# Spreading a step's softmax weights over the features: a full-precision product of 2 rows becomes a single-pass product of 34 rows

## The chip, the cores and the metric

The kernel runs on one core of a Trainium2 chip. The metric is the device time of one execution, in microseconds. The core's engines each run their own instruction stream and meet through semaphores: PE (TensorE) multiplies matrices, ACT (ScalarE) and DVE (VectorE) do elementwise work, POOL (GpSimd) builds constants and biases, SP starts transfers.

## The reference, cut to what matters

The program is a chain of transformer layers (two in the first block, two in the second) over 512 tokens of width 1024. The change touches one mixer only, the sparse attention of the first block's second layer. Each of its 16 heads attends in three ways, and a gate for each token and head weighs the three results:

```python
    o_c = jnp.einsum('ghqn,ngd->qghd', p_c, vc)      # 31 compressed keys
    ...
    o_s = jnp.einsum('ghqk,gqkd->qghd', p_s, v_sel)  # selected blocks
    ...
    o_w = jnp.einsum('ghqk,kgd->qghd', p_w, vw)      # window
    g = g_blk.astype(jnp.float32)
    o = g[..., 0:1] * o_c + g[..., 1:2] * o_s + g[..., 2:3] * o_w
```

Here every `p` is a softmax: exponentials divided by their sum. With 512 tokens there are only 8 blocks of 64, so all of them are selected, and both `o_s` and `o_w` are causal attention over all earlier keys.

## The kernel before, in words

All of x stays on chip, transposed (features on the partitions, 512 tokens along the row). Weights arrive in pieces of 128x2048; ACT rounds each to the single-pass format fp32r (L294) and DVE takes the rest (L300), so that a product of nearly full precision is three single-pass products (L304 to L306). Most of the program is such products.

The sparse attention works in 16 steps (`STEPS`), two for each pair of heads: an even step `n` for the selected branch, an odd one for the window. The loop in `pe_nsa`, `act_nsa` and `dve_nsa` runs over `n` and four query tiles `i`, and is pipelined by hand: in round `n` the scores of step `n` are made while the probabilities of step `n-1` are turned and multiplied by the values, and the end of step `n-2` is combined.

- PE: `scores` (L1281) writes a bank, DVE adds the bias and takes the maximum (`masked`, L1510), ACT takes the exponential with its sum (`exps`, L1423). PE turns the probabilities (L1309), ACT and DVE copy them back (L1432, L1559), PE multiplies by the values (`values`, L1325).
- The probabilities aren't normalized. `weigh` (DVE, L1546 to L1550) turns the sums into reciprocals times the gate, two columns of `mt` for the pair's two heads. `turn_small` (PE, L1334) transposes `mt` into bank 7, `take_small` (ACT, L1441) copies it into `ms`, `spread` (PE, L1339) multiplies by the 0/1 matrix `pick`, which repeats each head's row over its 64 features, and `take_spread` (ACT, L1449) copies the result into `oadd`. `combine` (DVE, L1564 to L1571) multiplies the values' product by it and adds.
- For an even step `mt` also holds the compressed branch's 64 columns (`weigh_cmp`, L1533 to L1541, fed by ACT's L1458), so that `take_small` copies 66 rows there and 2 rows for an odd step. PE then multiplies the compressed values with them (`values_cmp`, L1344).

The order on each engine is the order of the code. Two kinds of round alternate. In a round with odd `n`, `spread` serves an odd step (2 rows copied) and DVE also does the compressed branch's weights. In a round with even `n`, `spread` serves an even step (66 rows copied). The output projection (`out_part`, L304 to L306) is woven into the last two rounds.

Of the kernel before, what the change touches and what calls it, by code (L numbers as in the profile page):

```python
# [15 lines left out]
F32R = mybir.dt.float32r  # L16
ACT = mybir.ActivationFunctionType
ALU = mybir.AluOpType
AX = mybir.AxisListType

P = 128
# [3 lines left out]
QT = S // P  # L25
# [5 lines left out]
HEADS, HD, GROUPS = 16, 64, 4  # L31
CMP_LEN, CMP_STRIDE = 32, 16
NC = S // CMP_STRIDE - 1
# [8 lines left out]
def build(nc, a, out):  # L42
    ctx = ExitStack()
    with ctx:
        def sb(name, shape, dt=F32):
            return ctx.enter_context(nc.sbuf_tensor(name, shape, dt))

        def sem(name):
            return ctx.enter_context(nc.semaphore(name))
# [10 lines left out]
        u_hi = nc.alloc_sbuf_tensor_at("u_hi", [P, 4, S], F32R, offset=zone + 16 * S * 4)  # L60
        u_lo = nc.alloc_sbuf_tensor_at("u_lo", [P, 4, S], F32R, offset=zone + 20 * S * 4)
        fsum = sb("fsum", [P, KT, S])
        tmp = sb("tmp", [P, 8, S])
        ident = sb("ident", [P, P])
# [6 lines left out]
        arena = sb("arena", [P, AR])  # L71
        pbank = [ctx.enter_context(nc.psum_tensor(f"bank{i}", [P, S], F32)) for i in range(8)]

        def tiles(at, n, w=S):
            return arena[:, at:at + n * w].rearrange("p (t n) -> p t n", n=w)
# [42 lines left out]
        def chain(ins):  # L118
            act_chain(ins)
# [183 lines left out]
        def three(pe, o, w_hi, w_lo, r_hi, r_lo, first, last):  # L303
            pe.matmul(o, w_hi, r_hi, start=first, stop=False)  # L304
            pe.matmul(o, w_hi, r_lo, start=False, stop=False)  # L305
            return pe.matmul(o, w_lo, r_hi, start=False, stop=last)  # L306
# [788 lines left out]
        mt_dve, mt_pe, ms_act, rr_pe = sem("mt_dve"), sem("mt_pe"), sem("ms_act"), sem("rr_pe")  # L1095
# [3 lines left out]
        o = 0  # L1099
# [18 lines left out]
        rr = arena[:, o:o + 8]; o += 8  # L1118
        bias_h = (tiles(o, 2), tiles(8 * S, 2)); o += 2 * S
        osum, oadd = arena[:, 10 * S:11 * S], arena[:, 11 * S:12 * S]  # L1120
        cs = arena[:, o:o + 8 * (NC + 1)].rearrange("p (h q n) -> p h q n", h=2, q=QT); o += 8 * (NC + 1)
        mt = tiles(o, QT, 2 * (NC + 1) + 2); o += QT * (2 * (NC + 1) + 2)
        pick = arena[2 * (NC + 1):2 * (NC + 1) + 2, o:o + P]; o += P
        csT = arena[:, o:o + S]; o += S
        ms = csT
        cmx = arena[:, o:o + 8]; o += 8
# [13 lines left out]
        VR = 2 * (NC + 1)  # L1140
# [17 lines left out]
        def head_of(n, hd):  # L1158
            return 8 * (n // 2 // 4) + 4 * hd + n // 2 % 4

        def slope_of(h):
            return 2.0 ** (-8.0 * (h + 1) / HEADS)
# [26 lines left out]
        def pool_nsa(e, stage, chain):  # L1189
            e.wait_ge(n_sum, norm_no[stage])  # L1190
            chain(e.memset(tmp[:, :, :], 0.0))
            for h in range(2):
                r = slice(h * HD, h * HD + HD)
                e.dma_start(w1bd[1][r, :, r], NSA_SMALL[1][0][0].rearrange("(l d) e -> d l e", d=HD)).then_inc(small_in, 16)
            e.memset(mt[:, :, :], 0.0)
            chain(e.memset(gz[:, :, NC:NC + 1], 0.0))
            chain(e.memset(pick, 1.0))
            chain(e.affine_select(out=pick, in_=pick, compare_op=ALU.is_ge, fill=0.0, base=0, pattern=[[1, P]],
                                  channel_multiplier=-HD))
            chain(e.affine_select(out=pick, in_=pick, compare_op=ALU.is_ge, fill=0.0, base=HD - 1, pattern=[[-1, P]],  # L1200
                                  channel_multiplier=HD))
            for j in range(PAIRS):
                if j == 1:
                    e.wait_ge(na_dve, 3)
                if j >= 2:
                    e.wait_ge(sc_dve, unit_no[2 * j - 3, 3, 1] + 1)
                for hd in range(2):
                    ins = e.tensor_scalar(bias_h[j % 2][:, hd, :], dist, slope_of(head_of(2 * j, hd)), None, ALU.mult)
                ins.then_inc(bias_pool, 1)
# [3 lines left out]
        def pe_nsa(pe, stage):  # L1213
# [21 lines left out]
            for z in range(2):  # L1235
                ins = pe.transpose(pbank[1][:, z * 32:z * 32 + 32], perow[0:CMP_LEN, z, :], ident[0:32, 0:32])
            ins.then_inc(na_pe, 1)
            pe.wait_ge(na_dve, 1)
            for k in range(KT):
                gk = slice(k * 48, k * 48 + 48)  # L1240
                ins = three(pe, pbank[0][0:48, :], u_hi[:, 0, gk], u_lo[:, 0, gk], h_hi[:, k, :], h_lo[:, k, :], k == 0,
                            k == KT - 1)
            ins.then_inc(na_pe, 1)
            for z in range(2):
                o62 = pbank[2 + z][:, 0:2 * NC].rearrange("p (t n) -> p t n", t=2)
                pe.wait_ge(na_dve, 2 + z)
                for l in range(CMP_LEN):
                    src = (zA, zB)[l // CMP_STRIDE][z]
                    ins = pe.matmul(o62, w1bd[z][:, l, :], src[:, :, l:l + CMP_STRIDE * (NC - 1) + 1:CMP_STRIDE],
                                    start=l == 0, stop=l == CMP_LEN - 1)  # L1250
                ins.then_inc(na_pe, 1)
                if z == 0:
                    pe.wait_ge(na_act, 3)
                    for q in range(QT):
                        ins = pe.transpose(pbank[6][:, q * 48:q * 48 + 48], gT[:, q * P:q * P + P], ident[0:48, 0:48])
# [4 lines left out]
                else:  # L1260
                    pe.wait_ge(na_act, 6)
                    pe.wait_ge(bias_pool, 1)
                    for hd in range(2):
                        r = slice(hd * HD, hd * HD + HD)
                        for t2 in range(2):
                            ins = pe.matmul(pbank[5 + hd][32 * hd:32 * hd + 32, t2 * P:t2 * P + P], gz[r, t2, :], w2bd[r, 1, :],
                                            start=True, stop=True)
# [61 lines left out]
            def turn_small(n):  # L1329
                pe.wait_ge(mt_dve, n + 1)  # L1330
                if n:
                    pe.wait_ge(rs_act, n)
                for q in range(QT):
                    ins = pe.transpose(pbank[7][0:VR + 2, q * P:q * P + P], mt[:, q, :], ident[:, :])  # L1334
                ins.then_inc(mt_pe, 1)

            def spread(n):
                pe.wait_ge(ms_act, n + 1)
                pe.matmul(pbank[7][:, :], pick, ms[VR:VR + 2, :], start=True, stop=True).then_inc(rr_pe, 1)  # L1339

            def values_cmp(n):
                v = unit_no[n, "o"]
# [44 lines left out]
        def act_nsa(e, chain):  # L1387
# [44 lines left out]
                e.activation(probT[hd][:, c:c + nw], pbank[3 + hd][:, 0:nw], ACT.Copy).then_inc(done_, 1)  # L1432

            def take_small(n):
                r = slice(VR * (n % 2), VR + 2)
                e.wait_ge(mt_pe, n + 1)
                if n:
                    e.wait_ge(rr_pe, n)
                if n >= 2 and n % 2 == 0:
                    e.wait_ge(sc_pe, unit_no[n, "o"] + 1)  # L1440
                e.activation(ms[r, :], pbank[7][r, :], ACT.Copy).then_inc(ms_act, 1)  # L1441

            def take_spread(n):
                e.wait_ge(rr_pe, n + 1)
# [26 lines left out]
        def dve_nsa(e, stage, chain):  # L1471
# [17 lines left out]
            for z in range(2):  # L1489
# [3 lines left out]
                for half, dst in ((0, zA[z]), (1, zB[z])):  # L1493
                    for t in range(2):
                        pos = peT[:, z, half * CMP_STRIDE:(half + 1) * CMP_STRIDE].unsqueeze(1)
                        ins = e.tensor_tensor(dst[:, t, :].rearrange("p (n l) -> p n l", l=CMP_STRIDE),
                                              zc[:, 2 * z + t, :].rearrange("p (n l) -> p n l", l=CMP_STRIDE),
                                              pos.broadcast_to([P, S // CMP_STRIDE, CMP_STRIDE]), ALU.add)
# [28 lines left out]
            def gates_of(n, b):  # L1527
                c = 3 * head_of(n, 0) + b
                return gates[:, :, c:c + 13:12]
# [14 lines left out]
            def weigh(n):  # L1544
                e.wait_ge(ex_act, 8 * n + 8)
                chain(e.tensor_scalar(rr, sums[:, n % 2, :], 1e-30, None, ALU.max))  # L1546
                chain(e.reciprocal(rr, rr))
                if n:
                    e.wait_ge(mt_pe, n)
                e.tensor_tensor(mt[:, :, VR:VR + 2], rr.rearrange("p (q h) -> p q h", h=2), gates_of(n, 1 + n % 2),  # L1550
                                ALU.mult).then_inc(mt_dve, 1)

            def take_turned(n, g):
                nw = sum(QT - k for k in GROUPS[g]) * P
# [64 lines left out]
        o = AR - 8 * S - 104  # L1619
# [17 lines left out]
        o = 14 * S  # L1637
# [1133 lines left out]
        def _(pool):  # L2771
            chain = Chain(pool, pool_step)
            for stage, step in enumerate(PLAN):
                enter(pool, stage)
                if step[0] == "setup":
                    pool_setup(pool, chain)
                elif step[0] == "rg":
                    pool_rg(pool)
                elif step[0] == "nsa":
                    pool_nsa(pool, stage, chain)  # L2780
                elif step[0] == "even":
                    pool_even(pool, chain)
                elif step[0] == "odd":
                    pool_odd(pool)
                elif step[0] == "post":
                    pool_owed(pool, stage)
                elif step[0] == "ffn" and FFN[step[1]]["swiglu"]:
                    pool_ffn(pool, step[1])
                elif step[0] == "norm":
                    pool_norm(pool, stage)  # L2790
                    nxt = PLAN[stage + 1]
                    if nxt[0] == "ffn" and FFN[nxt[1]]["swiglu"]:
                        pool.wait_ge(n_add, 7 * norm_no[stage] + 7)
                        pool.memset(fsum[:, :, :], 0.0).then_inc(cleared, 1)
                    if nxt == ("ffn", "f0"):
                        pool_nsa_early(pool, chain)
                    elif nxt == ("ffn", "s00"):
                        pool_even_early(pool, chain)
                    elif nxt == ("ffn", "s10"):
                        pool_odd_early(pool, chain)  # L2800
                leave(pool, "pool")
# [97 lines left out]
```

## Time and profile before

| | us |
|---|---|
| median of 3 runs | 3739.74 |
| lowest and highest | 3736.36 and 3741.02 |
| profiled execution, its time | 3735.31 |
| profiled execution, its span | 3733.6 |
| PE busy | 3529.7 (95%) |
| DVE busy | 1919.1 (51%) |
| ACT busy | 1236.3 (33%) |

The span runs from the first to the last instruction of the trace; the time has a little around it (1.7 us here). A busy share is an average over the whole program; what a change of one stage is worth is read in that stage.

### The profile page before, as it was taken

The page shows a single profiled execution, that of the slowest core. Times are in us where ns is not written, and L with a number is a line of the kernel's source. Part 1 is how long each engine was busy: PE and PEld are TensorE (multiplying, and loading weights), DVE is VectorE, ACT ScalarE, POOL GpSimd, SP SyncE. Part 2 cuts the span into 40 slices and gives each one's busy share as a digit, 9 for nine tenths or more (in the row PEclk, how much of TensorE's full clock was granted, in tenths as well). Part 3 has the DMA queues.
Part 4 walks back from the last instruction along what each step waited for, and adds up shares of the span by engine and source line. Part 5 has one row for each costly group of instructions (what it writes and reads, how often), then busy time and mean ns, then how long its engine had stood idle before and what let it go on. Part 6 is the DMA issues. An engine that isn't in the chain of part 4 may idle for free.

```text
span 3733.6 us, 47718 instructions
## 1 busy us (share of the span) xinstructions
PE 3529.7 (95%) x18695; PEld 2801.1 (75%) x18695; DVE 1919.1 (51%) x2613; ACT 1236.3 (33%) x1717; POOL 512.7 (14%) x400
## 2 busy tenths in 40 slices
PE   6999999899999999999988799999999999989998
PEld 5788888545888878887666678877887777767886
DVE  5655554365555554554566444455445333344455
ACT  3632232365322342223633332233223323232222
POOL 1220002010100041113023021113111100012111
PEclk9999999899999999999999999999999999989999
DMA  3232334100223323232100122232332222212321
GB/s 103 88 107 90 101 98 105 34 1 10 92 90 101 101 81 101 90 101 85 57 25 3 46 79 96 95 101 69 100 101 91 79 79 79 79 57 90 101 90 68
DMA packets 232527, 295.54 MB, mean 79 GB/s; under 512 B 21893, under 2 KB 201464, under 8 KB 232392
## 3 DMA queue, kind: packets, MB, share of 16 engines
q1 hardware_dynamic: 230864, 290.48, 24.2%
q0 software_dynamic: 1152, 3.05, 0.4%
q8 instruction: 96, 1.57, 0.2%
q14 instruction: 39, 0.32, 0.0%
q10 hardware_dynamic: 376, 0.12, 0.0%
HBM read 291.53 MB, written 2.10 MB: 79 GB/s over the span
## 4 chain that ended last, share of the span: by engine, by line
PE 81%; DVE 8%; ACT 5%; issue 3%; POOL 2%; POOLq 0%; DMA 0%; ACTq 0%; DVEq 0%
PE bank L304 23%; PE bank L305 23%; PE bank L306 23%; POOL tmp L636 1%; PE bank L334 1%; PE bank L335 1%; PE bank L333 1%; ACT whi L294 1%; ACT h_hi L550 1%; PE bank L2639 1%; DVE x L681 1%; PE bank L2158 1%; DVE h_lo L665 1%; PE bank L1281 1%; PE bank L1325 1%
## 5 line engine op out<-in xcount | busy, mean ns | idle before, releaser
L304 PE MATMUL bank<-h_hi,whi 128*128 128x512 f32 x2800 | 1118.1, 399 | 53.7 <-DVE h_lo L665 38.2
L305 PE MATMUL bank<-h_lo,whi 128*128 128x512 f32 x2800 | 1101.1, 393 | 0.0
L306 PE MATMUL bank<-h_hi,wlo 128*128 128x512 f32 x2800 | 1100.5, 393 | 0.0
L294 ACT ACTIVATE whi<-raw 128x2048 fp32r<-128x2048 f32 x273 | 521.7, 1911 | 1342.8 <-PE bank L306 1288.3
L300 DVE TENSOR_TENSOR wlo<-raw,whi 128x2048 fp32r<-128x2048 f32 x273 | 632.3, 2316 | 445.6 <-ACT whi L294 445.3
L304 PEld LDWEIGHTS bank<-h_hi,whi 128*128 128x128 f32 x2800 | 533.4, 190 | 186.2 <-issue 71.9
L305 PEld LDWEIGHTS bank<-h_lo,whi 128*128 128x128 f32 x2800 | 533.6, 191 | 114.5 <-issue 5.7
L306 PEld LDWEIGHTS bank<-h_hi,wlo 128*128 128x128 f32 x2800 | 532.4, 190 | 113.2
L304 PE MATMUL bank<-u_hi,whi 128*128 128x512 f32 x1376 | 539.6, 392 | 26.8 <-DVE wlo L300 10.5
L306 PE MATMUL bank<-u_hi,wlo 128*128 128x512 f32 x1376 | 538.6, 391 | 0.0
L305 PE MATMUL bank<-u_lo,whi 128*128 128x512 f32 x1376 | 538.4, 391 | 0.0
L304 PEld LDWEIGHTS bank<-u_hi,whi 128*128 128x128 f32 x1376 | 260.6, 189 | 84.3 <-DVE wlo L300 11.4
L445 POOL TENSOR_TENSOR tmp<-tmp,rstd 128x512 f32<-128x512 f32 x88 | 175.5, 2015 | 1068.1 <-ACT tmp L414 1067.8
L305 PEld LDWEIGHTS bank<-u_lo,whi 128*128 128x128 f32 x1376 | 260.5, 189 | 54.2
L306 PEld LDWEIGHTS bank<-u_hi,wlo 128*128 128x128 f32 x1376 | 260.0, 189 | 54.6
L499 DVE TENSOR_TENSOR fsum<-fsum,bank 128x512 f32<-128x512 f32 x352 | 235.5, 685 | 92.6 <-PE bank L306 92.6
L499 DVE TENSOR_TENSOR x<-x,bank 128x512 f32<-128x512 f32 x256 | 169.6, 684 | 51.0 <-PE bank L306 50.9
L480 DVE TENSOR_TENSOR tmp<-bank,tmp 128x512 f32<-128x512 f32 x88 | 60.9, 692 | 253.1 <-PE bank L306 236.2
L465 DVE TENSOR_TENSOR tmp<-bank,rstd 128x512 f32<-128x512 f32 x88 | 60.1, 691 | 216.3 <-PE bank L306 215.3
L422 ACT ACTIVATE u_hi<-tmp 128x512 fp32r<-128x512 f32 x88 | 55.7, 633 | 336.5 <-DVE tmp L480 336.5
L469 DVE SCALAR_TENSOR_TENSOR tmp<-bank,rstd 128x512 f32<-128x512 f32 x64 | 44.1, 692 | 180.8 <-PE bank L306 180.8
L426 ACT ACTIVATE tmp<-tmp 128x512 f32<-128x512 f32 x64 | 40.5, 632 | 257.2 <-DVE tmp L469 257.2
(398 smaller groups left out, 3048.7 us busy)
## 6 DMA issues: line engine op xcount, KB each, us to landing
raw<-in_ffn_wgu SPq DMA_DIRECT2D x88, 1024.0 KB, 5.0
raw<-in_ffn_wd SPq DMA_DIRECT2D x44, 1024.0 KB, 4.9
raw<-in_mlp_w_up SPq DMA_DIRECT2D x32, 1024.0 KB, 5.3
raw<-in_mlp_w_down SPq DMA_DIRECT2D x32, 1024.0 KB, 5.0
raw<-in_odd_w_in SPq DMA_DIRECT2D x24, 1024.0 KB, 5.1
raw<-in_even_w_in SPq DMA_DIRECT2D x13, 1024.0 KB, 5.3
raw<-in_rg_w_in SPq DMA_DIRECT2D x8, 1024.0 KB, 5.3
raw<-in_odd_w_out SPq DMA_DIRECT2D x8, 1024.0 KB, 5.0
```

Source lines behind the costliest of these rows:

```text
L294: e.activation(whi[:, n % 2, :], raw[:, n % 2, :], ACT.Copy).then_inc(hi_ready, 1)
L300: e.tensor_tensor(wlo[:, n % 2, :], raw[:, n % 2, :], whi[:, n % 2, :].bitcast(F32), ALU.subtract).then_inc(lo_ready, 1)
L304: pe.matmul(o, w_hi, r_hi, start=first, stop=False)
L305: pe.matmul(o, w_hi, r_lo, start=False, stop=False)
L306: return pe.matmul(o, w_lo, r_hi, start=False, stop=last)
L422: e.activation(u_hi[:, u, :], tmp[:, 2 + j, :], ACT.Copy).then_inc(uhi_done, 1)
L426: e.activation(tmp[:, 2 + j, :], tmp[:, j, :], ACT.Square)
L445: e.tensor_tensor(tmp[:, j, :], tmp[:, j, :], rstd[:, :], ALU.mult).then_inc(scaled, 1)
L465: ins = e.tensor_tensor(tmp[:, j, :], pbank[half + j][:, :], rstd[:, :], ALU.mult)
L469: ins = e.scalar_tensor_tensor(tmp[:, j, :], pbank[half + j][:, :], 0.0, rstd[:, :], ALU.max, ALU.mult)
L480: e.tensor_tensor(tmp[:, 2 + j, :], pbank[half + 2 + j][:, :], tmp[:, j, :], ALU.mult)\
L499: e.tensor_tensor(dst[:, m, :], dst[:, m, :], pbank[half + m % 4][:, :], ALU.add)\
```

## The change

The weights are split as the big matrices are: DVE writes the rounded value (fp32r) of each of the two columns into `mt`, and what is left of it into the next column. To have each head's pair of rows beside each other, head 0 has columns `VR` and `VR+1`, head 1 has `VR+32` and `VR+33`; `mt` grows from 66 to 98 columns, and the columns between are zero. `pick` has ones in those four rows and zeros elsewhere, as fp32r, in a free part of `u_lo`. ACT copies 34 rows as fp32r into a free part of `u_hi`, and PE's product takes 34 rows of fp32r operands in one pass. The compressed branch's 64 rows are still copied as full fp32 into `ms`, by an instruction of their own in the even steps.

```diff
--- before.py
+++ after.py
@@ -1119,8 +1119,10 @@
         bias_h = (tiles(o, 2), tiles(8 * S, 2)); o += 2 * S
         osum, oadd = arena[:, 10 * S:11 * S], arena[:, 11 * S:12 * S]
         cs = arena[:, o:o + 8 * (NC + 1)].rearrange("p (h q n) -> p h q n", h=2, q=QT); o += 8 * (NC + 1)
-        mt = tiles(o, QT, 2 * (NC + 1) + 2); o += QT * (2 * (NC + 1) + 2)
-        pick = arena[2 * (NC + 1):2 * (NC + 1) + 2, o:o + P]; o += P
+        mt = tiles(o, QT, 2 * (NC + 1) + 34); o += QT * (2 * (NC + 1) + 34)
+        mt_r = mt.bitcast(F32R)
+        rw = arena[:, o:o + 8]; o += 8
+        pick, msr = u_lo[:, 3, 0:P], u_hi[:, 3, :]
         csT = arena[:, o:o + S]; o += S
         ms = csT
         cmx = arena[:, o:o + 8]; o += 8
@@ -1194,11 +1196,12 @@
                 e.dma_start(w1bd[1][r, :, r], NSA_SMALL[1][0][0].rearrange("(l d) e -> d l e", d=HD)).then_inc(small_in, 16)
             e.memset(mt[:, :, :], 0.0)
             chain(e.memset(gz[:, :, NC:NC + 1], 0.0))
-            chain(e.memset(pick, 1.0))
-            chain(e.affine_select(out=pick, in_=pick, compare_op=ALU.is_ge, fill=0.0, base=0, pattern=[[1, P]],
-                                  channel_multiplier=-HD))
-            chain(e.affine_select(out=pick, in_=pick, compare_op=ALU.is_ge, fill=0.0, base=HD - 1, pattern=[[-1, P]],
-                                  channel_multiplier=HD))
+            pick_f = bias_h[0][:, 0, 0:P]
+            chain(e.memset(pick_f, 0.0))
+            for hd in range(2):
+                ins = e.memset(pick_f[VR + 32 * hd:VR + 32 * hd + 2, hd * HD:hd * HD + HD], 1.0)
+            chain(ins)
+            chain(e.tensor_copy(pick, pick_f))
             for j in range(PAIRS):
                 if j == 1:
                     e.wait_ge(na_dve, 3)
@@ -1331,12 +1334,12 @@
                 if n:
                     pe.wait_ge(rs_act, n)
                 for q in range(QT):
-                    ins = pe.transpose(pbank[7][0:VR + 2, q * P:q * P + P], mt[:, q, :], ident[:, :])
+                    ins = pe.transpose(pbank[7][0:VR + 34, q * P:q * P + P], mt[:, q, :], ident[:, :])
                 ins.then_inc(mt_pe, 1)
 
             def spread(n):
                 pe.wait_ge(ms_act, n + 1)
-                pe.matmul(pbank[7][:, :], pick, ms[VR:VR + 2, :], start=True, stop=True).then_inc(rr_pe, 1)
+                pe.matmul(pbank[7][:, :], pick[VR:VR + 34, :], msr[VR:VR + 34, :], start=True, stop=True).then_inc(rr_pe, 1)
 
             def values_cmp(n):
                 v = unit_no[n, "o"]
@@ -1432,13 +1435,14 @@
                 e.activation(probT[hd][:, c:c + nw], pbank[3 + hd][:, 0:nw], ACT.Copy).then_inc(done_, 1)
 
             def take_small(n):
-                r = slice(VR * (n % 2), VR + 2)
                 e.wait_ge(mt_pe, n + 1)
                 if n:
                     e.wait_ge(rr_pe, n)
                 if n >= 2 and n % 2 == 0:
                     e.wait_ge(sc_pe, unit_no[n, "o"] + 1)
-                e.activation(ms[r, :], pbank[7][r, :], ACT.Copy).then_inc(ms_act, 1)
+                if n % 2 == 0:
+                    e.activation(ms[0:VR, :], pbank[7][0:VR, :], ACT.Copy)
+                e.activation(msr[VR:VR + 34, :], pbank[7][VR:VR + 34, :], ACT.Copy).then_inc(ms_act, 1)
 
             def take_spread(n):
                 e.wait_ge(rr_pe, n + 1)
@@ -1545,10 +1549,12 @@
                 e.wait_ge(ex_act, 8 * n + 8)
                 chain(e.tensor_scalar(rr, sums[:, n % 2, :], 1e-30, None, ALU.max))
                 chain(e.reciprocal(rr, rr))
+                rwq = rw.rearrange("p (q h) -> p q h", h=2)
+                chain(e.tensor_tensor(rwq, rr.rearrange("p (q h) -> p q h", h=2), gates_of(n, 1 + n % 2), ALU.mult))
                 if n:
                     e.wait_ge(mt_pe, n)
-                e.tensor_tensor(mt[:, :, VR:VR + 2], rr.rearrange("p (q h) -> p q h", h=2), gates_of(n, 1 + n % 2),
-                                ALU.mult).then_inc(mt_dve, 1)
+                chain(e.tensor_copy(mt_r[:, :, VR:VR + 33:32], rwq))
+                e.tensor_tensor(mt[:, :, VR + 1:VR + 34:32], rwq, mt[:, :, VR:VR + 33:32], ALU.subtract).then_inc(mt_dve, 1)
 
             def take_turned(n, g):
                 nw = sum(QT - k for k in GROUPS[g]) * P
```

On ACT, at `take_small` of the step with 66 rows in steady state (the round's end, `exps` of query tile 3, then the copies of the turned tiles and the next round's start), there stood before:

```order
L1423 ACTIVATE tmp,arena<-tmp,arena 128x512
L1441 ACTIVATE arena<-bank 66x512
L1432 ACTIVATE tmp<-bank 128x384 x2
L1423 ACTIVATE fsum,arena<-fsum,arena 128x128 x2
L1449 ACTIVATE arena<-bank 128x512
```

and now:

```order
L1426 ACTIVATE tmp,arena<-tmp,arena 128x512
L1444 ACTIVATE arena<-bank 64x512
L1445 ACTIVATE u_hi<-bank 34x512
L1435 ACTIVATE tmp<-bank 128x384 x2
L1426 ACTIVATE fsum,arena<-fsum,arena 128x128 x2
L1453 ACTIVATE arena<-bank 128x512
```

One copy of 66 rows has become two, ahead of the two copies of turned tiles; in the other rounds one copy of 2 rows has become one of 34.

On DVE, at `weigh_cmp` and `weigh` in a round with odd `n` (after `masked` of query tile 1, L1510 before), there stood before:

```order
L1510 ISA arena 128x1
L1533 TENSOR_REDUCE arena<-arena 128x8
L1534 TENSOR_SCALAR arena<-arena 128x8
L1535 RECIPROCAL arena<-arena 128x8
L1537 TENSOR_TENSOR arena<-arena 128x8
L1541 TENSOR_TENSOR arena<-arena 128x4x31 x2
L1546 TENSOR_SCALAR arena<-arena 128x8
L1547 RECIPROCAL arena<-arena 128x8
L1550 TENSOR_TENSOR arena<-arena 128x4x2
L1559 COPY tmp<-bank 128x512
```

and now, from `weigh` on:

```order
L1550 TENSOR_SCALAR arena<-arena 128x8
L1551 RECIPROCAL arena<-arena 128x8
L1553 TENSOR_TENSOR arena<-arena 128x8
L1556 CAST arena<-arena 128x4x2
L1557 TENSOR_TENSOR arena<-arena 128x4x2
L1565 COPY tmp<-bank 128x512
```

Two small instructions are added between the product with the gate and the copy of the turned tile; each of the first four waits for the end of the one before it.

## Rows read from the trace of the kernel before

**Rows 1.** The page: busy time by engine, then the chain's shares by engine.

```profile
PE 3529.7 (95%) x18695; PEld 2801.1 (75%) x18695; DVE 1919.1 (51%) x2613; ACT 1236.3 (33%) x1717; POOL 512.7 (14%) x400
...
PE 81%; DVE 8%; ACT 5%; issue 3%; POOL 2%; POOLq 0%; DMA 0%; ACTq 0%; DVEq 0%
```

**Rows 2.** Busy time by stretch: length, PE busy, granted clock, DMA share, GB/s.

```profile
744.15:768.50 24.35, 22.05 (x137) 1.00 0.00 1
...
792.84:817.42 24.58, 23.34 (x137) 0.93 0.00 1
817.42:842.53 25.11, 23.55 (x136) 0.93 0.00 1
```

**Rows 3.** Groups by form, 703 to 925 us: busy, mean ns, idle before.

```profile
L1339 PE MATMUL bank<-arena 2*128 2x512 f32 x32 | 17.9, 640 | 4.0 <-ACT arena L1441 4.0
...
L1309 PEld LDWEIGHTS bank<-ident,tmp 128*128 128x128 f32 x80 | 9.8, 145 | 0.2 <-DVE tmp L1559 0.2
...
L1334 PEld LDWEIGHTS bank<-ident,arena 128*66 128x66 f32 x64 | 5.8, 112 | 13.0 <-issue 13.0
```

**Rows 4.** Timeline, start of an odd round: start, duration, engine, line.

```profile
743.67 0.87 ACT L1432 ACTIVATE tmp<-bank 128x384 f32<-128x384 f32 x2
...
744.15 1.12 PE L1339 MATMUL bank<-arena 2*128 2x512 f32 x2
...
745.20 0.87 PE L1325 MATMUL bank<-tmp,arena 128*64 128x256 f32 x8
...
746.48 0.39 ACT L1458 ACTIVATE arena<-arena 128x248 f32<-128x248 f32 x1
...
746.74 0.42 DVE L1510 CUSTOM_DVE_ANT_0 fsum<-bank,arena 128x256 f32<-128x256 f32 x1 [1.34 <-PE bank L1281]
...
747.43 0.41 DVE L1533 TENSOR_REDUCE arena<-arena 128x8 f32<-128x248 f32 x1
...
748.31 0.17 DVE L1537 TENSOR_TENSOR arena<-arena 128x8 f32<-128x8 f32 x1
748.52 0.49 DVE L1541 TENSOR_TENSOR arena<-arena 128x124 f32<-128x124 f32 x2
...
749.36 0.17 DVE L1550 TENSOR_TENSOR arena<-arena 128x8 f32<-128x8 f32 x1
749.45 0.69 DVE L1559 COPY tmp<-bank 128x512 f32<-128x512 f32 x1
```

**Rows 5.** Timeline, end of that round and start of the even one.

```profile
755.55 0.58 ACT L1441 ACTIVATE arena<-bank 66x512 f32<-66x512 f32 x1
...
756.03 0.85 ACT L1432 ACTIVATE tmp<-bank 128x384 f32<-128x384 f32 x2
...
756.18 1.12 PE L1339 MATMUL bank<-arena 2*128 2x512 f32 x2 [0.39 <-ACT arena L1441]
...
757.23 0.63 PEld L1325 LDWEIGHTS bank<-tmp,arena 128*64 128x64 f32 x8 [0.76 <-ACT tmp L1432]
...
758.77 0.42 DVE L1510 CUSTOM_DVE_ANT_0 fsum<-bank,arena 128x256 f32<-128x256 f32 x1 [2.29 <-PE bank L1281]
...
760.65 0.69 DVE L1559 COPY tmp<-bank 128x512 f32<-128x512 f32 x1 [0.57 <-PE bank L1309]
```

**Rows 6.** Timeline, the last two rounds, with the output projection.

```profile
915.14 0.40 PE L304 MATMUL bank<-h_hi,whi 128*128 128x512 f32 x1
...
915.37 0.40 PE L305 MATMUL bank<-h_lo,whi 128*128 128x512 f32 x1
...
917.31 0.29 PEld L1339 LDWEIGHTS bank<-arena 2*128 2x128 f32 x2 [0.36 <-issue]
...
918.36 0.87 PE L1325 MATMUL bank<-tmp,arena 128*64 128x256 f32 x8
```

**Rows 7.** Timeline of POOL, the constants and biases before the steps.

```profile
581.76 2.99 POOL L1208 TENSOR_SCALAR arena<-arena 128x512 f32<-128x512 f32 x2
691.68 2.95 POOL L1208 TENSOR_SCALAR arena<-arena 128x512 f32<-128x512 f32 x2 [106.93 <-DVE zadd L1496]
```

## The prediction, made before the result was known

> **What bounds the kernel now.** I read the page first: PE is busy for 95% of the span and holds 81% of the chain that ended last [rows 1]. That speaks for any cut of PE's work. But it is an average, and the change touches only the 220 us of the attention's steps. So I cut these by rounds: two rounds take 24.35 us, in which PE is busy 22.05 us (its modelled ends make that too much) [rows 2]. Then I read the timeline of two rounds for what ends each wait. There PE, ACT and DVE hand the lead to one another: in the middle of an odd round it is DVE's row of small instructions [rows 4], at a round's end it is ACT, for whose copy the product L1339 waits [rows 5], and only in the last two rounds, beside the output projection, does PE have work without a break [rows 6]. So the question is not what PE saves, but what stands in the way of each of the 16 products.
>
> **What PE saves.** The full-precision product is recorded as two instructions, 32 for 16 products, of 640 ns each [rows 3]. From its start to that of the next product it holds PE for 1.05 us (744.15 to 745.20 us) [rows 4]. A single-pass product of 512 columns follows the one before it after 0.23 us and is recorded with 0.40 us [rows 6]. That is the nearest row for the new one; the 34 rows instead of 2 lie on partitions, and the 128-row product has the same length. Two double passes go down to one: 1.05 us is 0.85 us for the columns (four times 0.21) and 0.20 us of handing over, so the new one holds PE for 0.21 + 0.20 = 0.41 us. The saving is 0.64 us, 16 times: 10.2 us at the most, and nothing at the least.
>
> The Trainium skill ("FP8 and Floating Point Precision", the list of FP32 modes) says that true FP32 takes four passes through the array. By it the product is 4 x 0.21 us, which agrees with the 1.05 us once the handing over is taken off.
>
> **What ACT adds.** For an even step one copy becomes two. The copy of 66 rows is recorded with 0.58 us, and the next starts 0.48 us after its start [rows 5]. A copy of 64 or 34 rows has the same columns, so I take 0.48 us for the second; ends: 0.4 us, and 0.58 us if the two don't overlap. For odd steps 2 rows become 34 at the same columns, which I cost at nothing.
>
> **What DVE adds.** `weigh` gets two instructions of 8 elements. The product with the gate, L1550, now has to be waited for; before, the copy of the turned tile started 0.09 us after it (749.36 to 749.45 us). A waited-for one of that size, L1537, lets the next start after 0.21 us (748.31 to 748.52 us) [rows 4]. So the three now take 0.21 + 0.20 + 0.09 = 0.50 us where one took 0.09 us: 0.41 us more in each step. Ends: 0.25 us if the rounded copy is cheap, 0.6 us if writing columns 32 apart or the other format slows them.
>
> By the Trainium skill ("VectorE: DVE Perf Modes", the section on the TRN2 errata) a DVE instruction on SBUF costs 58 cycles plus its elements at 0.96 GHz, 0.07 us for 8 elements, and many small tiles each pay the fixed part. That rule speaks against this change. The trace has 0.17 us for each such instruction, so the rule's figure is too small here and its advice holds more strongly; by its figure the two would add 0.14 us.
>
> **Odd rounds, 7 in steady state [rows 4].** L1339 does not wait for ACT's copy here. At 0.41 us it would end at 744.56 us. L1325 also needs the turned tiles of L1432, which end at 743.67 + 0.87 = 744.54 us, and a semaphore takes 0.05 us (755.55 + 0.58 to 756.18 us [rows 5]): it starts at 744.59 us instead of 745.20 us, 0.61 us early. The scores behind it and DVE's L1510, which waited 1.34 us for them, come as much earlier, at 746.13 us. Then DVE's L1533, 0.69 us behind, would start at 746.82 us; but it needs ACT's L1458, which doesn't wait for PE's product and stays at 746.48 + 0.39 us, plus 0.05: 746.92 us. That is 0.51 us before its 747.43 us. From there on DVE leads without a gap up to L1559, and pays the 0.41 us. Gain: 0.51 - 0.41 = 0.10 us. Queued behind DVE are L1559, `combine` and the next L1510, for which ACT and PE wait, so the rest of the round moves with it.
>
> **Even rounds, 8 [rows 5].** Here L1339 does wait for ACT's copy (0.39 us). Its rows are now the second copy's: it starts 0.48 us later, at 756.66 us, and would let L1325 start at 757.07 us. But behind ACT's copies stand the two copies of turned tiles, L1432: they end 0.48 us later too, at 756.88 + 0.48 = 757.36 us, and L1325 starts at 757.41 us instead of 757.23 us. Loss: 0.18 us. What PE saved is eaten by the extra copy. DVE's 0.41 us lie here in the 0.57 us for which L1559 waits for PE's turned tile, so they cost nothing; with that cover gone they would cost 8 x 0.41 = 3.3 us.
>
> **The last round.** PE's stream is full (0.36 us of issue ahead of L1339, no engine named) and ACT's copy is long done [rows 6]. The projection moves up by the whole 0.64 us.
>
> **The transposes.** `turn_small` loads 98 columns of weights for 66. A load of 66 takes 112 ns, one of 128 takes 145 ns [rows 3], so about 15 ns more, four times a step, hidden in most steps by the bank that PE's scores wait for: 0 to 0.06 us a step, at most 1 us; I take 0.2 us. POOL's constants are made before 582 us, and its next work waits 107 us: nothing [rows 7].
>
> **The sum.** 8 x 0.18 - 7 x 0.10 - 0.64 + 0.2 = +0.3 us. The profiled 3735.31 us become 3735.6 us. That execution lay 4.4 us under the median of 3739.74 us, a tenth of a percent; against the median the forecast is 3740.0 us. No change: less than 0.2% (7.5 us) is about what a measurement of this kernel can't tell from none.
>
> **The rivals.**
>
> *PE's saving comes through everywhere.* If the even rounds' copies were hidden and DVE's two instructions too, all 16 products would give 0.64 us: -10.2 us, 3729.5 us. PE's 81% of the chain [rows 1] speaks for it; against it, that L1339 waits for ACT in the even rounds [rows 5] and that DVE runs without a gap in the odd ones [rows 4]. If only DVE's part is hidden, the odd rounds gain 7 x 0.41 us more: +0.3 - 2.9 = -2.6 us, 3737.1 us, still no change. Faster by over 0.2%: 4%.
>
> *The added small instructions win (still no change).* If DVE's 0.41 us are uncovered in the even rounds too, or the copies cost their upper ends: 3.3 us, or 8 x 0.10 us, more: up to 3744 us. 10%.
>
> *The clock falls (the other side).* The steps are a stage in which PE loses its full clock at times. Two pairs of rounds show a granted clock of 0.93, some time at 1.2 GHz instead of 2.4, and lasted 24.58 and 25.11 us instead of 24.35 us: 0.23 and 0.76 us lost [rows 2]. A lighter PE stream, 1.3 us less of 22.05 us in a pair, could make such falls more frequent. One more in each of the 5 pairs without one costs 1.2 to 3.8 us: 3741 to 3744 us. It is slower by over 0.2% only if each of the 16 rounds falls at the dearer price, less what has been paid: 16 x 0.76 - 1.0 = 11 us, 3751 us. Against it: the product's 2 rows are replaced, not removed, and PE stays busy for over 20 of 24 us. 6% for the dear form, 10% for the cheap one.
>
> The Trainium skill ("TensorE: Matmul & The Clock Gate", the section on what is actually happening) says that the throttled clock is the default and that activity releases it, and so speaks for this rival; the trace's falls come in some pairs and not in others with the same instructions, so the rule doesn't tell how many there would be.
>
> **How the numbers follow.** My case, gains and losses within 1.5 us of each other: 70%. The two small costs, still no change: 20%. Faster 4%, slower 6%. The range of 80% takes in DVE's part hidden (-2.6 us), the cheap falls of the clock (+3.8 us) and the runs' own spread (3736.36 to 3741.02 us): 3734 to 3745 us. Same: 90%.
>
> **What would show it.** The new product should be 16 instructions of about 0.4 us, and PE's busy time in the steps some 10 us lower. In odd rounds DVE's first small reduction should follow ACT's exponential and no longer PE; in even rounds L1325's counterpart should wait for ACT's copy by name, and DVE's wait for the turned tile should shrink from 0.57 to about 0.2 us. Pairs of rounds should take 24.4 to 24.5 us. I am wrong if a pair takes 23.5 us (the copy or DVE's chain didn't hold) or over 25 us in each (clock, or a chain dearer than its rows).

## The result and the profile after

The changed kernel took 3760.45 us (median of 4 runs, 3755.0 to 3763.5) against 3738.05 us for the kernel before (3734.34 to 3741.02, 4 runs). The ratio is 1.0059, with a 95% interval of 1.0041 to 1.0076: slower, by 15 to 28 us. The forecast was 3740.0 us, range 3734 to 3745 us, and no change.

The profiled execution took 3755.0 us. The first part of its page, busy time by engine, to be held against [rows 1]:

```profile
PE 3538.5 (94%) x18679; PEld 2809.4 (75%) x18679; DVE 1924.9 (51%) x2645; ACT 1241.8 (33%) x1725; POOL 510.1 (14%) x401
```

It tells nearly nothing: PE is busy 9 us longer although its products got lighter. The stretches tell more. Two rounds, from one product of an odd round to the next; length, busy time and count of PE, PEld, DVE, ACT and POOL, granted clock, DMA share, GB/s (as [rows 2]):

```profile
744.69:772.75 28.06, 23.91 (x136) 12.65 (x135) 16.96 (x63) 16.36 (x48) 3.35 (x2) 0.88 0.00 1
772.75:800.60 27.85, 23.94 (x136) 12.55 (x135) 16.97 (x63) 16.36 (x48) 3.36 (x2) 0.88 0.00 1
```

A pair of rounds took 24.35 us and now takes about 28 us, at a mean granted clock of 0.88 instead of 1.00. From the first of the 16 products to the last it is 728.13 to 942.80 us, 214.7 us; before it was 728.82 to 917.31 us, 188.5 us. So the stage lost 26.2 us in this execution, and the rest of the program, which the change doesn't touch, was 7 us shorter than in the other profile. That is no more than executions of the kernel before differ from each other, and is left unexplained. Here are pieces of 4 us of PE in one even round (length, PE busy, granted clock, DMA share, GB/s):

```profile
752.00:756.00 4.00, 3.68 (x22) 1.00 0.00 0
756.00:760.00 4.00, 2.49 (x19) 0.95 0.02 4
760.00:764.00 4.00, 4.00 (x14) 0.50 0.00 0
764.00:768.00 4.00, 4.00 (x17) 0.69 0.00 0
768.00:772.00 4.00, 4.00 (x34) 1.00 0.00 0
```

PE does 2.49 us of work in 4 us, and then its clock is 1.2 GHz instead of 2.4 for nearly 7 us, in which it is busy throughout (the three pieces lack 0.05, 0.50 and 0.31 of the full clock, and at half the clock 0.5 is lacking: 4 x 0.86 / 0.5 = 6.9 us). A fall follows the product in every even round. PE's busy time in such a piece doesn't tell by itself where a fall comes, for the next odd round has a piece with as little work, and no fall behind it:

```profile
776.00:780.00 4.00, 2.51 (x14) 1.00 0.00 0
780.00:784.00 4.00, 3.67 (x22) 1.00 0.00 0
```

The timeline of the even round at 756 us shows what PE waited for (as [rows 5]; start, duration, engine, line, idle before):

```profile
756.42 0.57 ACT L1444 ACTIVATE arena<-bank 64x512 f32<-64x512 f32 x1
...
757.01 0.59 ACT L1445 ACTIVATE u_hi<-bank 34x512 fp32r<-34x512 f32 x1
...
757.62 0.87 ACT L1435 ACTIVATE tmp<-bank 128x384 f32<-128x384 f32 x2
757.65 0.18 PEld L1342 LDWEIGHTS bank<-u_hi,u_lo 34*128 34x128 f32 x1 [1.20 <-ACT u_hi L1445]
757.65 0.49 PE L1342 MATMUL bank<-u_hi,u_lo 34*128 34x512 f32 x1 [1.01 <-ACT u_hi L1445]
...
758.64 0.87 PE L1328 MATMUL bank<-tmp,arena 128*64 128x256 f32 x8 [0.49 <-ACT tmp L1435]
```

The product waits 1.01 us for ACT where it waited 0.39 us, and the next one waits 0.49 us more. L1435 begins 1.20 us after L1444; one copy took 0.48 us before. The second copy was priced at 0.48 us and cost 0.72 us. Two groups of the trace, 703 to 945 us (busy, mean ns, idle before), to be held against [rows 3]:

```profile
L1342 PE MATMUL bank<-u_hi,u_lo 34*128 34x512 f32 x16 | 7.8, 487 | 9.3 <-ACT u_hi L1445 9.3
...
L1337 PEld LDWEIGHTS bank<-ident,arena 128*98 128x98 f32 x64 | 6.5, 131 | 14.0 <-issue 14.0
```

The product itself is what was forecast, 16 instructions of half a microsecond. The load of 98 columns takes 131 ns, 19 more.

### The profile page after: what moved, and what is told of

It reads as the page before. It is cut to its first block, busy times and chain, and to the rows that moved or that the text cites. A ratio compares the mean times of both kernels' runs of the same rounds, so it can differ in the third digit from the quotient of the medians.

```text
span 3752.9 us, 47727 instructions
## 1 busy us (share of the span) xinstructions
PE 3538.5 (94%) x18679; PEld 2809.4 (75%) x18679; DVE 1924.9 (51%) x2645; ACT 1241.8 (33%) x1725; POOL 510.1 (14%) x401
## 4 chain that ended last, share of the span: by engine, by line
PE 81%; DVE 8%; ACT 5%; issue 3%; POOL 2%; POOLq 0%; DMA 0%; ACTq 0%; DVEq 0%
PE bank L304 23%; PE bank L305 23%; PE bank L306 23%; POOL tmp L636 1%; PE bank L335 1%; PE bank L333 1%; PE bank L334 1%; ACT whi L294 1%; PE bank L1284 1%; ACT h_hi L550 1%; PE bank L2645 1%; DVE x L681 1%; PE bank L2164 1%; PE bank L1328 1%; DVE h_lo L665 1%
```

## The experiments

Two theories stood after the result. A: the lighter PE stream is itself what lets the clock fall. B: the work added to ACT or DVE costs the time, and the clock only follows. Every kernel below was run beside the kernel before, whose median was 3735.47 us beside e1 to e4, 3735.91 us beside e5 to e8 and 3737.43 us beside e9 to e12. The ratio's 95% interval stands in brackets; the ratio can differ a little from the quotient of the two medians.

### One part of the change at a time

**e1, the single-pass product alone.** The weights are rounded and their low part is left out; one copy of 66 rows, all rounded.

```diff
-                pe.matmul(pbank[7][:, :], pick, ms[VR:VR + 2, :], start=True, stop=True).then_inc(rr_pe, 1)
+                pe.matmul(pbank[7][:, :], pick[VR:VR + 2, :], msr[VR:VR + 2, :], start=True, stop=True).then_inc(rr_pe, 1)
...
-                e.activation(ms[r, :], pbank[7][r, :], ACT.Copy).then_inc(ms_act, 1)
+                e.activation(msr[r, :], pbank[7][r, :], ACT.Copy).then_inc(ms_act, 1)
```

> The kernel before with only the product changed: one pass on 2 rows of rounded weights; the low part of the weights is left out, ACT still makes one copy of 66 rows (all rounded), DVE's weigh is that of before. Theory A (the clock: a lighter PE stream in the even rounds lets TensorE fall to 1.2 GHz there): falls in most pairs of rounds, granted clock 0.83 to 0.89 over 704 to 924 us, time 3748 to 3758 us although no engine got more work. Theory B (the time went into ACT's and DVE's added instructions, the clock only follows): neither is there, so the product's 0.6 us in odd rounds come through, clock 0.93 as before, 3729 to 3735 us.

Measured: 3726.47 us against 3735.47 us, 0.9972 (0.9959 to 0.9986). Faster. A stretch of two of its rounds:

```profile
741.00:764.62 23.62, 20.87 (x135) 10.94 (x133) 16.35 (x59) 15.53 (x47) 3.35 (x2) 1.00 0.00 1
```

PE has 1.2 us less work in this pair than before, and its clock stays at 2.4 GHz. Over the 16 products the granted clock is 0.98, where it was 0.96. Theory A falls. The pair takes 0.73 us less than [rows 2] shows, 0.51 us of which was worked out for the odd round.

**e2, ACT's second copy alone.** The product, in full precision, and DVE are those of before.

```diff
-                r = slice(VR * (n % 2), VR + 2)
...
+                if n % 2 == 0:
+                    e.activation(ms[0:VR, :], pbank[7][0:VR, :], ACT.Copy)
-                e.activation(ms[r, :], pbank[7][r, :], ACT.Copy).then_inc(ms_act, 1)
+                e.activation(ms[VR:VR + 2, :], pbank[7][VR:VR + 2, :], ACT.Copy).then_inc(ms_act, 1)
```

> The kernel before with only ACT's copy of 66 rows split into one of 64 and one of 2 in the even steps. Theory A: the product waits 0.6 us longer in 8 rounds, and nothing else: 3742 to 3746 us, clock at 0.91 to 0.93. Theory B: most of the 22 us is here: 3750 us or more.

Measured: 3779.67 us, 1.0112 (1.0088 to 1.0136): 44 us from eight copies of 0.6 us, twice what the whole change costs. A stretch of two rounds, and the product's wait:

```profile
747.29:777.99 30.70, 28.20 (x137) 14.17 (x135) 16.31 (x59) 16.44 (x49) 3.35 (x2) 0.78 0.00 1
```

```profile
760.49 0.59 ACT L1442 ACTIVATE arena<-bank 2x512 f32<-2x512 f32 x1
...
761.13 1.32 PE L1339 MATMUL bank<-arena 2*128 2x512 f32 x2 [0.99 <-ACT arena L1442]
```

The same wait of 1 us as in the changed kernel, and a clock of 0.78. Why it falls lower here than in the changed kernel (0.88), with the same wait, no run shows.

**e3, DVE's two small instructions alone.** `weigh` writes its product aside, copies it, and copies it again into `mt`.

```diff
+                chain(e.tensor_tensor(rwq, rr.rearrange("p (q h) -> p q h", h=2), gates_of(n, 1 + n % 2), ALU.mult))
...
+                chain(e.tensor_copy(rz_, rw))
+                e.tensor_copy(mt[:, :, VR:VR + 2], rz_.rearrange("p (q h) -> p q h", h=2)).then_inc(mt_dve, 1)
```

> The kernel before with only two more small instructions of 8 elements on DVE in each step, chained as in the changed kernel. Theory A: 0.4 us in the odd rounds, 3740 to 3743 us, clock at 0.93. Theory B: 3745 us or more, with 0.4 to 0.8 us in every round.

Measured: 3741.86 us, 1.0017 (1.0 to 1.0034), 6 us more at the median, and not clear of nothing by the interval. The first pair, at full clock, took 24.99 us (744.22 to 769.21 us) where 24.35 us were before. Of these 0.64 us, 0.23 us are a single gap, which the later rounds don't have:

```profile
748.38 0.17 DVE L1539 TENSOR_TENSOR arena<-arena 128x8 f32<-128x8 f32 x1
748.82 0.48 DVE L1543 TENSOR_TENSOR arena<-arena 128x124 f32<-128x124 f32 x2 [0.27 <-DVE arena L1539]
```

The other 0.41 us are the two instructions, all in the odd round; the even one took 12.32 us as before. That is some 3 us in seven pairs. The rest of the 6 us may be the clock's: of 40 pieces of 4 us, from 744 to 904 us, 12 had a granted clock below 0.95, where the kernel before had 4.

**e4, as many columns as before on PE.** The changed kernel issues its product four times into the same bank.

```diff
+                for _ in range(3):
+                    pe.matmul(pbank[7][:, :], pick[VR:VR + 34, :], msr[VR:VR + 34, :], start=True, stop=True)
```

> The changed kernel with its single-pass product issued four times over into the same bank (the result is the same), so that PE streams as many columns as in the kernel before. Theory A: the falls of the clock go back to the few of before, the granted clock in the steps returns to about 0.93, and the time falls to 3741 to 3750 us, below the changed kernel's 3760 although PE does more. Theory B: PE's added 0.64 us a round come on top or are hidden: 3760 to 3770 us.

Measured: 3764.92 us, 1.0088 (1.0071 to 1.0104), no better than the changed kernel. Its row shows why:

```profile
785.19 0.96 PE L1343 MATMUL bank<-u_hi,u_lo 34*128 34x512 f32 x3 [1.01 <-ACT u_hi L1447]
```

The wait of 1.01 us stands ahead of the product, and columns behind it don't fill it. Of the 40 pieces 12 lie below 0.95, 14 in the changed kernel: the columns themselves did little. This too speaks against theory A.

### Taking ACT's copy or PE's wait away

**e5, the changed kernel with one copy.** One of 98 rows, all rounded; the low part of the compressed branch's weights is left out.

```diff
...
-                if n % 2 == 0:
-                    e.activation(ms[0:VR, :], pbank[7][0:VR, :], ACT.Copy)
-                e.activation(msr[VR:VR + 34, :], pbank[7][VR:VR + 34, :], ACT.Copy).then_inc(ms_act, 1)
+                r = slice(VR * (n % 2), VR + 34)
+                e.activation(msr[r, :], pbank[7][r, :], ACT.Copy).then_inc(ms_act, 1)
```

> The changed kernel with ACT's two copies of an even step made one again, of 98 rows, all rounded; the low part of the compressed branch's weights is left out. Product and DVE work are those of the changed kernel. If ACT's second copy is the cause (the product waits 1.0 us for it instead of 0.4 us, and the clock falls behind that wait): the falls go, granted clock in the steps 0.92 to 0.96, 3728 to 3740 us. If the single-pass product or DVE's two instructions are the cause: 3752 us or more.

Measured: 3731.33 us against 3735.91 us, 0.9983 (0.997 to 0.9996). The whole loss is gone, with PE's and DVE's parts of the change still there.

**e6, the copy of 64 rows on DVE.** The full arithmetic of the change; PE's product waits for both copies.

```diff
...
-                if n % 2 == 0:
-                    e.activation(ms[0:VR, :], pbank[7][0:VR, :], ACT.Copy)
...
+                        if n % 2 and n <= STEPS:
+                            e.wait_ge(mt_pe, n)
...
+                            e.tensor_copy(ms[0:VR, :], pbank[7][0:VR, :]).then_inc(ms_dve, 1)
```

> The changed kernel with the copy of the 64 rows made by DVE after query tile 3, where it waited 0.6 us, instead of by ACT. All arithmetic is that of the changed kernel. If ACT's second copy is the cause: 3730 to 3742 us, with at most 0.3 us a pair for DVE's 0.7 us copy. If not: as the changed kernel, 3755 us or more.

Measured: 3734.37 us, 0.9999 (0.9987 to 1.001): equal to the kernel before. A pair with a fall of the clock, and one at full clock:

```profile
769.00:794.91 25.91, 22.30 (x137) 11.52 (x135) 17.54 (x64) 15.79 (x47) 3.36 (x2) 0.93 0.00 1
845.17:869.50 24.33, 20.78 (x136) 11.01 (x135) 17.64 (x64) 15.77 (x47) 3.36 (x2) 1.00 0.00 1
```

**e7, the changed kernel with PE's wait filled.** All three parts stay; ahead of the product of an even step (seven of the eight) PE multiplies the identity by itself four times into a free bank, and nothing reads it.

```diff
+                if n % 2 == 0:
+                    v = unit_no.get((n + 2, 1, 0), 0)
+                    if v:
+                        free_bank(v)
+                        for _ in range(4):
+                            pe.matmul(pbank[v % 3][:, 0:P], ident[:, :], ident[:, :], start=True, stop=True)
```

> The changed kernel, with four products of the identity by itself on PE ahead of the product in even rounds, into a free score bank, about 0.9 us of work in the 1.0 us that PE waits for ACT's copy; they are thrown away. If it is PE's idle stretch that lets the clock fall: granted clock up from 0.84 to 0.93 or more, and the time falls to the full clock's own sum, 3738 to 3746 us. If the clock isn't decisive, or the stretch isn't: 3755 us or more.

Measured: 3741.09 us, 1.0016 (1.0006 to 1.0025). PE does more, no other engine does less, and of 22 us over the kernel before 5 are left. The fillers in place of the wait, and a pair of rounds:

```profile
753.44 1.16 PE L1346 MATMUL bank<-ident 128*128 128x128 f32 x8
754.53 0.49 PE L1348 MATMUL bank<-u_hi,u_lo 34*128 34x512 f32 x1
```

```profile
766.60:791.39 24.79, 21.79 (x144) 11.98 (x143) 17.05 (x63) 16.24 (x48) 3.36 (x2) 1.00 0.01 1
```

24.79 us is taken below for what a pair of the changed kernel takes at full clock. Its own trace has no whole pair without a fall, but its odd half agrees: 12.73 us (772.75 to 785.48 us) against 12.72 us here.

**e8, the same fillers in e2.**

The lines are those of e7, put into e2.

> The kernel before with only ACT's copy split (3780 us so far) and the same four fillers. If the idle stretch lets the clock fall: 3740 to 3750 us. If the delay itself costs the time: 3775 us or more.

Measured: 3742.39 us, 1.001 (1.0001 to 1.002), 6 us over the kernel before, where e2 was 44 us over it: 38 of the 44 us were the clock's. So theory B has the place right, ACT's second copy, and not the way: the work itself costs 5 to 6 us in either kernel, and the fall of the clock behind PE's wait costs the rest. What exactly makes the clock fall is open.

### Why the second copy cost 0.72 us and not 0.48

**e9, the kernel before with the copy of 66 rows made twice, both from row 0.**

```diff
+                if n % 2 == 0:
+                    e.activation(u_hi[r, 3, :], pbank[7][r, :], ACT.Copy)
```

> The kernel before with the copy of 66 rows made twice in the even steps, both from row 0 on (the first into a place that nothing reads). In the kernel with the split copy, 64 rows and then 2 rows from row 64 on, the two took 1.2 us from the first's start to the next instruction's, against 0.48 us for one. If a copy that begins at row 64 is what overlaps with nothing: here 0.96 us (2 x 0.48), the product waits 0.87 us instead of 0.99, and falls of the clock are fewer: 3745 to 3770 us. If every second copy of that bank costs 0.6 us: 1.2 us again and 3775 to 3782 us.

Measured: 3762.4 us, 1.0079 (1.0051 to 1.0107). ACT's timeline, first in an odd step and then in an even one:

```profile
743.22 0.59 ACT L1443 ACTIVATE arena<-bank 2x512 f32<-2x512 f32 x1
743.83 0.87 ACT L1432 ACTIVATE tmp<-bank 128x384 f32<-128x384 f32 x2
756.93 0.57 ACT L1442 ACTIVATE u_hi<-bank 66x512 fp32r<-66x512 f32 x1
757.40 0.58 ACT L1443 ACTIVATE arena<-bank 66x512 f32<-66x512 f32 x1
757.88 0.85 ACT L1432 ACTIVATE tmp<-bank 128x384 f32<-128x384 f32 x2
```

Two copies that begin at row 0 follow one another after 0.47 us, and the next instruction after 0.48 us. The copy of 2 rows, which begins at row 64, gives way after 0.61 us, and in e2 the one ahead of it after 0.59 us. So an instruction and its neighbour that begin at different partitions didn't overlap here, and the number of rows isn't what matters: 66 rows and the 128 rows behind them overlap, and in the changed kernel the copy of 64 rows from row 0 begins at 756.42 us, before the instruction ahead of it ends (756.52 us). The product waits 0.87 us here. A copy of 0.48 us still makes the clock fall, less often: 25 us lost and not 44.

### Looking for a better order on DVE

In odd rounds DVE's small instructions stand ahead of the masked scores for which ACT waits 3 us. Three kernels changed only DVE's order (e12 with one more wait, for `o_lo`, ahead of `combine`'s product in even rounds); e10 and e11 start from e6, e12 from the kernel before.

```diff
 e11 and e12:
-                            weigh(n - 1)
-                        take_turned(n - 1, i - 1)
+                    if i == 1 and 1 <= n <= STEPS:
+                        take_turned(n - 1, 0)
                     if i == 1 and n >= 2:
                         combine(n - 2)
+                    if i == 2 and 1 <= n <= STEPS:
+                        if n % 2:
+                            weigh_cmp(n - 1)
+                        weigh(n - 1)
+                        take_turned(n - 1, 1)
```

> The changed kernel with the 64 rows copied by DVE, and on DVE the first copy of turned tiles ahead of the weights' small instructions. If DVE's total sets the odd round: the same 3734 us within 4. If PE's wait for that copy (1.15 us) is what ends late: 0.5 us or more in each odd round, 3726 to 3731 us.

> The same with the weights made after the scores of query tile 2 are masked, instead of before. If ACT and PE wait for the masked scores behind the small instructions (ACT waited 3.5 us there): about 1 us less in each odd round, 3722 to 3730 us. If the late transpose of the weights holds PE instead: 3735 us or more.

> The kernel before, with its full-precision product, and that order on DVE. It tells what is the order's and what the change's: if the single-pass product is worth 0.5 us in each of the 16 rounds once nothing else leads, this one is 4 to 8 us slower than the changed one in the same order; if not, equal within 3 us.

Measured: e10, with only the first `take_turned` moved ahead of the weights, 3744.15 us, 1.0007 (0.9988 to 1.0026), no gain that shows, and in its trace a pair at full clock takes 25.28 us where e6 takes 24.33 us; e11 3761.34 us, 1.0059 (1.0039 to 1.0079); e12 3756.41 us, 1.0056 (1.0033 to 1.008). The gains expected of e10 and e11 as one of two outcomes didn't come: e10 lies above both of its ranges, and in e11 the other outcome came. In e11 the masked scores do come earlier, and PE's transpose of the weights pays for it:

```profile
781.96 0.64 PE L1338 MATMUL bank<-ident,arena 128*98 128x128 f32 x4 [2.43 <-DVE arena L1556]
```

A wait of 2.43 us on PE, and a clock at half speed behind it. e12 has the same order with the product of before and lies as high as e11 (1.0056 and 1.0059), so in this order the whole change brought nothing that can be measured; e11 also has DVE's copy and its two small instructions, so the product's own part isn't told apart. No kernel with the full arithmetic was faster than the kernel before.

## Why the prediction was wrong

**The bounds, and the rounds.** Where it looked was right: the stage is a hand-over between three engines, and PE's saving is worth what stands behind it. The 10.2 us of the page's view never came. Its own sign of being wrong did: every pair took over 25 us.

**PE's saving: right.** The product is 16 instructions of 0.49 us, and where nothing else is late it holds PE for 0.42 us (942.80 to 943.22 us, the last one), with 0.41 us forecast and 1.05 us before. Alone it gains 9 us (e1). At full clock that is 0.73 us in each of seven pairs, 0.53 us of it in the odd and 0.20 us in the even round, and 0.63 us at the end: 5.7 us. The even rounds gain since without the second copy the turned tiles let L1325 go up to 0.3 us earlier [rows 5]. The rest is not taken apart; the clock, 0.98 for 0.96 over the 16 products in e1's trace, can be a part of it.

**Odd rounds: right.** The changed kernel's later pairs show each step of it:

```profile
775.26 0.40 ACT L1462 ACTIVATE arena<-arena 128x248 f32<-128x248 f32 x1
...
775.69 0.41 DVE L1537 TENSOR_REDUCE arena<-arena 128x8 f32<-128x248 f32 x1
...
778.13 0.68 DVE L1565 COPY tmp<-bank 128x512 f32<-128x512 f32 x1
```

From the scores ahead of the product (L1284 at 772.50 us) to DVE's L1565 it is 5.63 us; before (L1281 at 743.73 us to L1559) it was 5.72 us. That is the forecast gain of 0.10 us: two small instructions ate the 0.5 us that PE gave. In even rounds they lay in DVE's wait for the turned tile, as forecast: it fell from 0.57 to 0.15 us, as e7 shows at full clock:

```profile
783.71 0.69 DVE L1571 COPY tmp<-bank 128x512 f32<-128x512 f32 x1 [0.15 <-PE bank L1312]
```

**Even rounds: the term was mis-sized.** The step "I take 0.48 us for the second" failed: it was 0.72 us, since the copies begin at different partitions and neither overlaps with its neighbour (e9), 0.14 us beyond even the upper end of 0.58 us. The trace of the kernel before had a row for it, in an odd round, where the copy begins at row 64 too; L1432 begins at 743.67 us [rows 4], 0.61 us after its start:

```profile
743.06 0.59 ACT L1441 ACTIVATE arena<-bank 2x512 f32<-2x512 f32 x1
```

The next product came 2.22 us after the first copy's start instead of 1.68 us: a loss of 0.54 us in each even round and not 0.18 us. Less the odd round's 0.10 us that is 0.44 us a pair, and just that shows at full clock: 24.79 us (e7) against 24.35 us, some 3 us over seven pairs.

**The clock: this is the step that decided.** The prediction named the fall of the clock as a rival, at 6% for the dear form, and argued against it that "PE stays busy for over 20 of 24 us". That argument is the step that failed. It is a mean over a pair, the same error that it warned of in the page's 95%. What counted was the product's wait at one place: it went from 0.39 to 1.01 us, and behind it the clock fell. Without the second copy (e5), with it on another engine (e6) or with the wait filled (e7, e8) most falls went. That the wait brings the falls is shown. By which rule is not: the piece before the fall had 2.49 us of work, but one with 2.51 us had no fall behind it, and with nearly the same wait the loss was 22 us in the change and 44 us in e2. It also named the wrong trigger, the lighter product: with that alone the clock stayed up (e1), and with the wait alone it fell most (e2). And its price was too low. It read 0.23 and 0.76 us from two short falls, early in odd rounds. Here most last nearly 7 us and cost 27.85 - 24.79 = 3.1 us in a pair. One was short, with a granted clock of 0.94 over its pair against 0.93 in those two, and cost 26.39 - 24.79 = 1.6 us behind the even round's product, so the place counts beside the length:

```profile
800.60:826.99 26.39, 22.35 (x137) 11.79 (x135) 16.97 (x63) 16.56 (x49) 3.36 (x2) 0.94 0.00 1
```

The seven pairs up to the last product took 198.1 us (744.69 to 942.80 us) where they took 173.2 us: 25 of the 26.2 us that the stage lost. 3 of them are work, by the pair at full clock, and 22 are what is left. The granted clock agrees: 0.13 of 198.1 us less 0.02 of 173.2 us is 22 us, if PE led wherever the clock was down. The first row is the changed kernel's, the second that of the kernel before:

```profile
744.69:942.80 198.11, 170.26 (x917) 90.61 (x915) 114.97 (x416) 110.68 (x315) 16.78 (x10) 0.87 0.00 1
744.15:917.31 173.16, 158.68 (x929) 81.26 (x927) 109.66 (x388) 105.49 (x308) 16.79 (x10) 0.98 0.00 1
```

The Trainium skill ("TensorE: Matmul & The Clock Gate", the section on HAM oscillation) describes a kernel whose waits throttle PE anew at every step of its loop. There the wait is a transfer's and longer than the products between two waits. The pattern is the same here, and the sizes are not: the wait is ACT's, 1.0 us in a pair of 28 us. The fillers of e7 and e8 show what it costs, 17 and 38 us.

**The transposes and POOL.** A load of 98 columns takes 19 ns more, where about 15 ns were forecast. Four times that is 0.08 us a step, a little over the upper end of 0.06 us, but hardly any of it shows: from the four transposes' start to PE's next instruction it is 0.57 us (780.36 to 780.93 us) where it was 0.55 us (751.68 to 752.23 us). POOL's first biases, behind its constants, begin at 580 us (582 us before), and its next work waited 107 us. Right.

## What to carry to other kernels

Ahead of TensorE a wait can cost more than its length, by what half a clock costs in the stretch behind it: 0.6 us added to eight waits cost 22 us in the change and 44 us in e2. A mean over a round or the page doesn't show it. So look at the waits of PE and at the granted clock in pieces of a few microseconds around the place where an edit adds a wait, and measure the wait alone, as e2 does; PE's busy time in such pieces didn't tell where the clock would fall. An instruction on another engine that feeds a product is part of that product's price; moving it to an engine that is idle just then (e6), or filling PE's wait with products that nothing reads (e7), brought nearly all of it back.

## What the runs showed of the hardware that was not expected

ACT's copies of 512 columns out of a bank took 0.57 to 0.59 us, with 2, 34, 64, 66 or 128 rows. A following instruction began 0.48 us after the start where both began at partition 0, and 0.59 to 0.61 us where one began at 64 (e2, e9).

More work on PE made the program faster: four thrown-away products in a pair of rounds, 1.1 us of them, took 38 us of e2's 44 away (e8). Columns added to the changed kernel behind the wait and not in it (e4) brought nothing: 3764.92 us.
